# A hybrid-attention decoder layer on one core: ten of the sixteen MoBA pairs beside the projection panels instead of nine, the last six spaced further apart

## The reference

```
z = x @ w_in                      # 19 slots of up to 128 columns, for 520 rows
A: GLU, causal depthwise conv, LayerNorm, swish, pointwise
B: compressed + selected + sliding-window attention (4 query heads, shared K/V)
C: MoBA, 4 heads: blocks of 256 keys, gate q . mean(k over block),
   top 3 past blocks plus the own block, softmax, p @ v
D: causal pooling, per-group map
x = LN(alpha*x + concat(A,B,C,D) @ w_out)
x = LN(alpha*x + relu(x @ w_up)^2 @ w_down)
```

## Time and profile before

| | |
|---|---|
| median of 3 runs | 768.91 us (768.2 to 770.05) |
| profiled execution, its own time | 771.64 us |
| its span, first to last instruction | 770.0 us |
| mean granted TensorE clock | 0.986 |
| TensorE busy | 95% of the span |
| VectorE, ScalarE, GpSimd busy | 56%, 37%, 27% |

### The profile page before, as it was taken

How to read it: one execution, slowest core, us unless ns; L and a number is a source line. 1 busy time by engine, 2 the same in 40 slices (tenths; PEclk the granted TensorE clock), 3 DMA queues, 4 the chain that set the end, 5 groups by cost and what they waited for, 6 DMA issues and landing times.

```text
span 770.0 us, 17310 instructions
## 1 busy us (share of the span) xinstructions
PE 734.7 (95%) x6888; PEld 656.8 (85%) x6888; DVE 432.7 (56%) x746; ACT 286.1 (37%) x561; POOL 205.7 (27%) x281
## 2 busy tenths in 40 slices
PE   9999999988988799999999999999999999999994
PEld 8999989866564346589999999999999999999993
DVE  4878994655644442556866556433563355536366
ACT  5222334555553232533434454212341134323125
POOL 0000527012235783003747721001110012100433
PEclk9999999999999999999999999999999999999997
DMA  9656773387698998321432333322233322325002
GB/s 342 172 154 181 207 211 93 146 278 277 220 299 302 251 304 239 119 83 56 137 137 83 87 105 103 117 83 83 83 105 92 106 75 91 110 83 165 1 15 98
DMA packets 63979, 113.47 MB, mean 147 GB/s; under 512 B 17017, under 2 KB 36218, under 8 KB 63226
## 3 DMA queue, kind: packets, MB, share of 16 engines
q1 hardware_dynamic: 57370, 95.58, 40.6%
q0 software_dynamic: 6528, 16.78, 6.4%
HBM read 107.90 MB, written 6.52 MB: 149 GB/s over the span
## 4 chain that ended last, share of the span: by engine, by line
PE 78%; DVE 10%; issue 4%; ACT 3%; SPq 3%; DMA 2%; POOL 0%; ACTq 0%; DVEq 0%; POOLq 0%
PE psum L788 55%; PE psum L807 4%; PE psum L815 3%; PE psum L894 2%; DMA moba_hi<-in_moba_pages 2%; PE psum L928 2%; PE psum L1093 2%; PE psum L1081 1%; PE psum L863 1%; DVE yc L1681 1%; SPq L705 1%; DVE wL L1611 1%; PE psum L942 1%; SPq L627 1%; DMA moba_lo<-in_moba_pages 1%
## 5 line engine op out<-in xcount | busy, mean ns | idle before, releaser
L1611 DVE TENSOR_TENSOR wL<-raw,wH 128x1024 fp32r<-128x1024 f32 (+1 forms) x87 | 109.5, 1260 | 89.2 <-ACT wH L1246 89.2
L1246 ACT ACTIVATE wH<-raw 128x1024 fp32r<-128x1024 f32 (+1 forms) x87 | 88.8, 1021 | 101.6 <-PE psum L788 100.5
L788 PE MATMUL psum<-oxH,wH 128*128 128x260 f32 (+1 forms) x512 | 105.0, 286 | 0.7 <-DVE oxL L2035 0.5
L788 PE MATMUL psum<-oxH,wL 128*128 128x260 f32 (+1 forms) x512 | 103.9, 284 | 0.0
L788 PE MATMUL psum<-oxL,wH 128*128 128x260 f32 (+1 forms) x512 | 103.4, 283 | 0.0
L1575 POOL TENSOR_TENSOR hsq<-relu 128x520 f32<-128x520 f32 x32 | 33.8, 1056 | 217.9 <-ACT relu L1425 217.9
L788 PE MATMUL psum<-opH,wH 128*128 128x260 f32 x400 | 85.9, 296 | 3.6 <-DVE wL L1611 1.4
L788 PEld LDWEIGHTS psum<-oxH,wH 128*128 128x128 f32 x512 | 79.5, 189 | 2.5 <-issue 1.7
L788 PE MATMUL psum<-opH,wL 128*128 128x260 f32 x400 | 81.5, 286 | 0.0
L788 PE MATMUL psum<-opL,wH 128*128 128x260 f32 x400 | 81.0, 285 | 0.0
L788 PEld LDWEIGHTS psum<-oxL,wH 128*128 128x128 f32 x512 | 79.9, 190 | 0.0
(11 more groups left out here) (387 smaller groups left out, 1300.5 us busy)
## 6 DMA issues: line engine op xcount, KB each, us to landing
raw<-in_panels SPq DMA_DIRECT2D x88, 512.0 KB, 3.6
nsa_ring<-in_nsa_pages SPq DMA_DIRECT2D x128, 96.0 KB, 2.2
moba_hi<-in_moba_pages SPq DMA_DIRECT2D x36, 256.0 KB, 5.1
moba_lo<-in_moba_pages SPq DMA_DIRECT2D x36, 256.0 KB, 4.7
moba_hi<-in_moba_pages POOLq DMA_DIRECT2D x28, 256.0 KB, 5.7
moba_lo<-in_moba_pages POOLq DMA_DIRECT2D x28, 256.0 KB, 5.3
xres<-in_xT SPq DMA_DIRECT2D x8, 260.0 KB, 4.9
xres<-in_xT SPq DMA_DIRECT2D x1, 2080.0 KB, 9.6
```

Source lines behind the costliest of these rows:

```text
L788: last = mm(out[:, hf, 0:cols], w, x[:, k, hf * HALF:hf * HALF + cols], start=(t == 0 and j == 0), stop=(t == KT - 1 and j == 2))
L1246: fn(wtiles(0, n).rearrange("p a b -> p (a b)")[:, cols], raw[:, n % NRAW, cols], ACT.Copy).then_inc(h_done, 1)
L1611: tt(wtiles(1, n).rearrange("p a b -> p (a b)")[:, cols], raw[:, n % NRAW, cols], wtiles(0, n).rearrange("p a b -> p (a b)")[:, cols].bitc ...
```

## The change

Three numbers change in one line; `SELV_T` stays.

```
-MB1, PAIR_T, SELV_T = 9, 9.1, 6
+MB1, PAIR_T, SELV_T = 10, 10.3, 6
```

## The result

The changed kernel takes 779.4 us (776.31 to 780.7, 5 runs), the kernel before, timed beside it, 770.03 us (768.2 to 770.73, 5 runs). The ratio is 1.0112, 95% interval 1.009 to 1.0135: slower by 1.1%. The forecast was 770.0 us.

The account below looks back on a forecast made before the run. Bound: TensorE, 95% busy, idling for pages in panel 16 and the tail's first third. Tail starts 6.3 us later, lasts 98.2 - 2.2 - 1.7 - 2.2 - 1.6 + 2.5 = 93.0: +1.1 us, put at 770.0; range 765.8 to 772.9.

Parts of the forecast that it names:

- The panel: Panel 16: tail starts 6.3 us later, at 240.0; 2.2 us is moved work, 4.1 us new waiting.
- the reload: Panel 16: time from a pair's `mp` end until the pages of the pair two further on arrive, 10.1 to 10.2 us.
- the last reload, pair 9's: End of panel 16: pair 9's pages take 8.9 us after pair 7's `mp`, arriving at 234.0; 2.1 us of wait.
- the lower bound of 5.0: Panel 16: with full clock at the end, the tail starts at 238.7, 5.0 us later than before.
- the stretch priced at 1.3 us: End of panel 16: half clock included in the 6.0 us from pair 9's `mu` to the end of its `mp`.
- a pair less: Tail: one pair's TensorE work moves to the panel, -2.2 us.
- the third pair's page wait: Tail: pages come as late as before but TensorE arrives 1.7 us later; wait shrinks from 2.44 to 0.7 us.
- the `PTm2` wait: Tail: VectorE's combine step now comes ahead of the third pair's reductions, so the 2.19 us wait goes, -2.2 us.
- its half clock gone: Tail: the half-rate stretch behind the `PTm2` wait goes too, -1.6 us.
- pair 13 at the queue: Tail's fourth pair: waits for pages issued behind 16 selV pages in SyncE's queue, +2.5 us, bounds 0.5 to 3.4.
- The clock rival: Panel and tail: more short gaps add half-rate stretches, +2.9 us on top of +1.1, 772.9 us; chance 30%.
- The faster rival: Tail gains more than panel loses: tail starts at 237.8 and lasts 91.5 us, total 766.3 us; chance 28%.

Follow-up runs that it names:

- the profile near the median: Second profile of the unaltered changed kernel, span 779.0 us, from timing it once more: median 780.37 us, ratio 1.0127 to the kernel before.
- small pages: MoBA pages from pair 2 on cut to 128 of 512 columns: changed kernel 765.19 us, kernel before 767.44 us.
- the first profile: Profiled execution of the changed kernel in its first timing, the shortest of five: 776.31 us, span 774.6 us.
- pages first: Changed kernel with SyncE issuing the selV pages of samples 0 and 2 behind the pages of pairs 12 and 13: 772.14 us, ratio 1.0013.
- spare matmuls: Changed kernel with 4, 5, 3 and 7 extra 128x128 matmuls ahead of the page waits of pairs 6 to 9: 775.73 us, ratio 1.0068.
- `spv` early: Changed kernel with each `spv` step planned 6.0 instead of 6.5 behind its sample's start: 775.4 us, ratio 1.0066.

## Why the prediction was wrong

The forecast had the tail start at 240.0 and panel 17 at 333.0. In the profile near the median they start at 242.22 and 341.03: 2.2 us were missed in the panel and 5.8 us in the tail. That what follows panel 17 does not change was right.

**The panel.** The mechanism was as described: the waits of pairs 7 to 9, the `mt` waits, and the reload as the bound, which small pages show by removing it. The step that failed is the last reload, pair 9's, taken as 8.9 us "since no third pair's pages compete for most of it". It took 11.1 us (224.15 + 1.0 to 236.26), and that is the whole 2.2 us: pair 7's `mp` was to end at 225.1 and ended at 225.15, and from pair 9's `mu` to the end of its `mp` 6.0 us were taken and 5.96 came. That pair 7 fits so well is partly luck, since pair 6 started 0.7 us later than taken and pair 7's pages 0.5 us sooner. Even the upper bound, 10.2 us, was too low. The reason given holds only for half of the time: pair 8's pages were under way until 227.38, and pair 10's were issued from 233.06 on.

In the first profile the tail starts 4.3 us later than before, under the lower bound of 5.0, by errors against each other: pair 9's reload took 10.1 us instead of 8.9, but pair 7 was through 1.6 us earlier than forecast, and without the half-rate stretch the steps from pair 9's `mu` on took 4.5 us instead of 6.0. So the stretch priced at 1.3 us is worth 1.5 us. It was in the forecast; it is not what was missed.

The page of the Trainium skill on "DMA: Bandwidth & Descriptors", section "Anatomy of one DMA — SWDGE (gpsimd) path", would put these 2 MB at 6.8 us, an estimate from its figure for one DMA issued from GpSimd, while half of a pair's pages goes by SyncE. The reloads of the panel, 8.6 us (pair 8, first profile: 215.89 + 1.0 to 225.46) to 11.1 us, do not agree.

**The tail.** Forecast 93.0 us; measured 98.6 and, in the profile near the median, 341.03 - 242.22 = 98.8 us. Term by term for the latter:
- a pair less, -2.2: right.
- the third pair's page wait from 2.44 to 0.7, -1.7: failed. It was 2.38. The step behind it, "the SyncE queue is the same relative to the tail's start", does not hold: its pages were issued 17.6 us behind the start before (251.25 - 233.7), and now 18.4 and 20.5 us behind (256.45 and 262.70).
- the `PTm2` wait, -2.2: right, 0.3 us is left.
- its half clock gone, -1.6: that stretch is gone, but two others of 0.68 and 0.66 over 5 us cost 1.6 and 1.7 us, where the forecast had none. So +1.7 instead of -1.6, the largest single error, 3.3 us.
- pair 13 at the queue, +2.5: right in kind and near in size, 2.0 us, though its pages were issued 33.7 us behind the start (275.94) instead of 30.7. In the first profile pair 12 waited 0.59 us, as forecast, and pair 13 3.85 us. Together the two waits are 4.4 us in both profiles, where 0.7 + 2.5 = 3.2 were forecast.
- missing: the waits for `PTw`, 2.0 us where 0.3 was, +1.7. The prediction put the rest of the tail at nothing because TensorE was busy there. It could be read from the order of the changed kernel; I had looked only at the places around the pairs.

These sum to -2.2 - 0.1 - 2.1 + 1.7 + 2.0 + 1.7 = +1.0 us, against 0.6 us measured. That the queue is the weak step is shown by changing nothing but its order: pages first brings the tail to 93.0 us. That this is the very number of the forecast is luck, since the `PTw` waits stay in it.

**The rivals.** The clock rival asked for a half-rate stretch more in the panel and one kept in the tail, +2.9 us. The panel had one, as in the forecast, and the tail two, +3.3 us: near in size, but without the reload, the page waits and the `PTw` waits it reaches only 772.9 us. It also counted the gaps of the old panel as 1.3 to 1.9 us, where the rows have 0.43 and 0.27 us among them.

By the rule that I cited with it (the Trainium skill, "TensorE: Matmul & The Clock Gate", section "A second HAM failure mode: psum-queue depth-cycling"), repeated short idling costs throughput each time. The granted clock of 0.50 and 0.54 in the second profile agrees, the 1.00 through like waits in the first does not, and where half-rate work lay ahead of a wait for pages, it cost nothing.

The faster rival's condition, a tail start below 238.5, was met in the first profile (238.03), and it was 776.3 us all the same, since the rival's tail of 91.5 us needed the queue to bring pair 13 early.

**Still open.** Why one execution keeps the clock through the panel and another does not; pair 9's wait is even the longer one, 3.06 us, where the clock stayed up. What makes a reload take anything from 8.6 to 11.1 us. And what share of the medians' 4.6 us of the spare matmuls and 5.0 us of `spv` early belongs to the edit.

## What to carry to other kernels

Before moving work beside another stage, ask what each stage's queue of DMA issues can carry: a wait saved ahead of a late issue is only waited for at it, so the sum of the gains is worth nothing until the last issue moves. When a planner's total length changes, compare its whole order, not only the steps that one means to move. And price a half-rate stretch only by the work behind the last wait that it reaches: of nearly 10 us at half clock 1.5 to 1.7 us were lost here, because the rest lay inside a reload that had to be waited for anyway. Where two executions of one kernel differ, compare them step by step before naming a cause.

## What the runs showed of the hardware

- Issuing the small pages held SyncE's queue longer than issuing the large ones: in the tails 16 DMAs of 32 KB took 9.41 to 12.28 us, 0.59 to 0.77 us each, and 4 of 256 KB mostly 1.88 us, 0.47 us each (up to 3.85). With three quarters of the MoBA bytes gone, the 16 still took 11.59 us. With four small pages in one DMA, four DMAs took 8.62 us at one place and 2.72 us at the next.
- The reload of 2 MB, four pages from SyncE and four from GpSimd, took 8.6 to 11.1 us in the last panel.
- With spare matmuls in front of its page waits panel 16 ran at a clock of 1.00 in all four kernels profiled so. Against pages first alone they made the steps behind the last page wait 1.7 us shorter.
- The same program kept the full clock through the panel's waits of 1.75, 0.66, 0.97 and 3.06 us in one execution, and lost it for nearly 10 us after 1.90, 1.40 and 1.26 us in another.
